# The first modulation split by column halves, and a reordered last head pair in two attention stages

## The reference, cut to what matters

```python
def _modulate(xn, shift, scale):
    return xn * (1.0 + scale) + shift
# first block: x and its context h, both 256 x 1024
ml = (jax.nn.silu(c) @ ada_w[l] + ada_b[l]).reshape(B, N_MOD, 1, D)      # 9 vectors of 1024
x = x + 0.5 * ml[:, 2] * _swiglu(_modulate(_rms(x, ffn1_norm[l]), ml[:, 0], ml[:, 1]), ffn1_w_in[l], ffn1_w_out[l])
...
# second block, twice: attention with 8 heads beside a gated recurrence and merge gates
o_a = nsa_attention(q_a, k_cmp, v_cmp, kv_a[:, :, 2], kv_a[:, :, 3], kv_a[:, :, 4], kv_a[:, :, 5], gates_a, rel_table)
log_a = jax.nn.log_sigmoid((a_lr @ gla_a_w2[l] + gla_a_b[l]).astype(jnp.float32)) / GLA_TAU
o_b = gla_attention(...)
o_b = o_b.reshape(B, S, GLA_HEADS * GLA_DV) * jax.nn.silu(r_b)
gm = jax.nn.sigmoid(g_merge).reshape(B, S, 2, D)
y = gm[:, :, 0] * (o_a @ w_branch_nsa[l]) + gm[:, :, 1] * (o_b @ w_branch_gla[l])
```

## Time and profile before

| what | value |
|---|---|
| median of 3 runs | 2425.76 us (2425.75 to 2430.88) |
| the profiled execution | 2424.43 us |
| its span in the trace | 2422.7 us |
| granted clock, mean | 0.994 |
| PE busy | 2351.5 us, 97% of the span |
| DVE, ACT busy | 1570.5 us (65%), 1162.6 us (48%) |

### The profile page before, as it was taken

The page is one execution under the profiler, slowest core; times in us unless marked ns, Lnnn a source line. Parts: engine busy times, 40 slices in busy tenths (PEclk is TensorE's granted clock), DMA queues, the critical chain, the costliest instruction groups (busy, mean ns, idle before and its releaser), DMA issues.

```text
span 2422.7 us, 33029 instructions
## 1 busy us (share of the span) xinstructions
PE 2351.5 (97%) x13342; PEld 1974.8 (82%) x13342; DVE 1570.5 (65%) x2355; ACT 1162.6 (48%) x1725; POOL 13.0 (1%) x43
## 2 busy tenths in 40 slices
PE   7999999999999999999999998999999999989998
PEld 4887787888888887888888887888888888878887
DVE  4686434656655686667766468676776665766766
ACT  4212323435533345445444478554454446874444
POOL 0000000000000000000000000000000000000000
PEclk9999999999999999999999999999999999999999
DMA  7467322323521224654455643345545555434553
GB/s 301 188 240 267 122 91 103 120 87 124 203 86 57 88 90 164 235 191 174 175 190 191 221 157 140 134 180 191 190 175 191 191 171 217 152 119 164 195 189 137
DMA packets 57920, 399.67 MB, mean 165 GB/s; under 512 B 7789, under 2 KB 8309, under 8 KB 10280
## 3 DMA queue, kind: packets, MB, share of 16 engines
q1 hardware_dynamic: 52704, 383.80, 43.4%
q10 hardware_dynamic: 4272, 10.08, 1.2%
q0 software_dynamic: 800, 3.73, 0.5%
HBM read 396.53 MB, written 2.63 MB: 165 GB/s over the span
## 4 chain that ended last, share of the span: by engine, by line
PE 85%; DVE 6%; ACT 6%; DMA 1%; issue 1%; SPq 0%; DVEq 0%; ACTq 0%
PE pair L506 80%; DMA ring<-in_stream 1%; DVE ring_parts L2294 1%; ACT mix_high L1562 1%; PE pair L901 1%; DVE ring_parts L2284 1%; ACT arena L1912 1%; PE pair L619 1%; PE pair L884 1%; PE pair L1039 1%; ACT ring_high L1549 1%; PE pair L1294 0%; PE pair L848 0%; DVE rows L2411 0%; DVE X L2417 0%
## 5 line engine op out<-in xcount | busy, mean ns | idle before, releaser
L506 PE MATMUL pair<-xT_parts,ring_high 128*128 128x512 f32 x2112 | 747.8, 395 | 4.2 <-DVE ring_parts L2284 1.1
L506 PE MATMUL pair<-xT_parts,ring_parts 128*128 128x256 f32 (+2 forms) x2448 | 694.6, 298 | 7.4 <-DVE ring_parts L2294 4.9
L2284 DVE TENSOR_TENSOR ring_parts<-ring,ring_high 128x2048 fp32r<-128x2048 f32 x194 | 444.1, 2292 | 142.1 <-ACT ring_high L1549 142.0
L506 PEld LDWEIGHTS pair<-xT_parts,ring_parts 128*128 128x128 f32 (+1 forms) x2448 | 461.5, 189 | 51.2 <-issue 12.1
L506 PEld LDWEIGHTS pair<-xT_parts,ring_high 128*128 128x128 f32 x2112 | 384.5, 188 | 81.8 <-DVE ring_parts L2284 2.7
L1549 ACT ACTIVATE ring_high<-ring 128x2048 fp32r<-128x2048 f32 x198 | 377.3, 1909 | 68.2 <-DMA ring<-in_stream 68.2
L2294 DVE TENSOR_TENSOR ring_parts<-ring,mix_high 128x1024 fp32r<-128x1024 f32 x144 | 168.5, 1219 | 77.6 <-ACT mix_high L1562 77.2
L1600 ACT ACTIVATE arena<-pair 128x512 f32<-128x512 f32 x110 | 65.5, 596 | 259.7 <-PE pair L506 259.6
L506 PE MATMUL pair<-ring_parts,xT_parts 128*128 128x512 f32 (+1 forms) x448 | 174.3, 389 | 0.2 <-DVE rows L2524 0.2
L1562 ACT ACTIVATE mix_high<-ring 128x1024 fp32r<-128x1024 f32 x144 | 143.1, 1047 | 61.6 <-DMA ring<-in_stream 57.7
L506 PE MATMUL pair<-ring_parts,g_high 128*128 128x512 f32 x440 | 171.8, 391 | 0.2 <-issue 0.2
(11 more groups left out here) (417 smaller groups left out, 3908.2 us busy)
## 6 DMA issues: line engine op xcount, KB each, us to landing
ring<-in_stream SPq DMA_DIRECT2D x338, 1024.0 KB, 4.8
xn<-in_mods SPq DMA_DIRECT2D x14, 1024.0 KB, 4.9
arena<-in_mods SPq DMA_DIRECT2D x14, 1024.0 KB, 4.9
arena<-in_bT ACTq DMA_DIRECT2D x1, 1536.0 KB, 8.9
bias_scratch<-bias_row POOLq DMA_DIRECT2D x1, 1536.0 KB, 8.3
X<-in_x ACTq DMA_DIRECT2D x1, 1024.0 KB, 11.9
X<-in_ctx ACTq DMA_DIRECT2D x1, 1024.0 KB, 16.4
arena<-in_bT ACTq DMA_DIRECT2D x1, 1024.0 KB, 7.3
```

What stands on the lines that cost most here:

```text
L506: m = pe.matmul(o, l, r, start=start, stop=stop)
L2284: dve.tensor_tensor(out=ring_r[:, slot].rearrange("p a b -> p (a b)"), in0=w, in1=high[:, slot, :], op=ALU.subtract).then_inc(low_ready, 1)
```

## The change

It has two parts that don't touch one another.

**The start.** X and its context are now the first transfers of SP's queue, ahead of the chunks. The first modulation is computed in two column halves, features 0 to 511 and 512 to 1023: four ring chunks hold the first half (two values of k and two of the groups in each), and four chunks of a new tensor, `late`, hold the second, loaded straight into the arena after the ring's fifth chunk. The first two up tiles are repacked so that chunk 0 holds slices 0 to 3 of both and chunk 1 slices 4 to 7 of both. PE runs: three chunks of the first half, slices 0 to 3 of X (`norm_wide`), the fourth chunk, the turn of half 0, slice 4, the first half of up tile 0, the four late chunks, the first half of up tile 1 with the turn of half 1 and the slices 5 to 7 in it, and the second halves of both tiles. ACT and DVE put the second half's work between slices 3 and 4.

**The attention.** In ACT's `beside` the split of a chunk comes after the take and what belongs to it where s is even, where it came before; in odd steps it stays. DVE's `operands` and memset move from step 5 to behind the `maxima` of the last pair.

```diff
@@ SP
+            sp.dma_start(X[:, 0:2, :], t["x"]).then_inc(inputs, 16)
+            sp.dma_start(X[:, 2:4, :], t["ctx"]).then_inc(inputs, 16)
             for j in range(SLOTS):
                 sp.dma_start(ring[:, j], t["stream"][j]).then_inc(loaded[j], 16)
...
+                for j in range(QUAD_LATE) if n == QUAD else ():
+                    sp.dma_start(late_w[j], t["late"][j]).then_inc(late_loaded[j], 16)
@@ PE
             def modulation():
                 pe.wait_ge(consts, FIRST_CONSTS)
                 pe.wait_ge(sc_done, 1)
-                for k in range(KD):
-                    if k == KD - 2:
-                        norm_wide(range(0, 2))
+                for c4 in range(QUAD):
+                    if c4 == QUAD - 1:
+                        norm_wide(range(0, 4))
                     chunk_wait(c.chunk)
-                    quad_part(0, k, ring[:, c.chunk % SLOTS], mod_full if k == KD - 1 else None)
+                    half_part(0, c4, ring[:, c.chunk % SLOTS])
                     owed.append(read[c.chunk % SLOTS])
                     c.chunk += 1
-                quad_turn(0)
+                half_turn(0)
+                norm_wide(range(4, 5))
...
+                def up_first(f, part):
+
+                    low_wait(part)
+                    for k in range(CW * part, CW * part + CW):
...
+                        if (f, k) == (1, 0):
+                            half_turn(1)
+                        if (f, k) == (1, 2):
+                            norm_wide(range(5, 8))
...
+                if nt == 4:
+                    up_first(0, 0)
+                    for j in range(QUAD_LATE):
+                        late_part(j)
+                    up_first(1, 0)
+                    up_first(0, 1)
+                    up_first(1, 1)
@@ ACT
                     for i in range(2):
                         n = 2 * (s % 2) + i
-                        mix_split(l, 16 + 2 * s + i)
+                        if s % 2:
+                            mix_split(l, 16 + 2 * s + i)
                         if s < 2:
                             values(n)
...
                             merge_gate_(n, r2, gm1_sig)
+                        if s % 2 == 0:
+                            mix_split(l, 16 + 2 * s + i)
@@ DVE
+            def second_ready():
+
+                first_half(1)
+                keep_half(1)
+                low(0, 1)
...
-                    elif s == 5:
-                        operands()
-                        step(dve.memset(PlL[:, :, :, :], 0.0))
...
                     for g in range(2):
                         maxima(j, g)
+                    if j == PAIRS - 1:
+                        operands()
+                        step(dve.memset(PlL[:, :, :, :], 0.0))
                     for g in range(2):
                         scale(j, g)
```

More of the change, by code:

```diff
@@ L28 @@
 MOD_STEPS = 18
+QUAD_LATE = 4
 SUMMED_AT = {8: 1, 12: 2, 14: 3, 18: 4}
@@ L291, in build @@
         unit_set = sem("unit_columns_set")
+        late_loaded = mod_loaded + [sem(f"late_modulation_chunk_loaded{i}") for i in range(2)]
         mod_full = sem("modulation_products")
@@ L613, in norm_wide @@
                 for k in slices:
-                    if k == 6 and slices.start:
-                        pe.wait_ge(mod_kept, 1)
+                    if k == 5 and slices.start:
+                        pe.wait_ge(mod_kept, 2)
                     for t_ in range(4):
@@ L703, in up_tile @@
                     steps = [(half, range(KD)) for half in range(2)]
-                    if f == 0 and nt == 4:
-                        steps = [(half, range(k, k + 1)) for k in range(KD) for half in range(2)]
-                    elif f == 0:
+                    if f == 0:
                         steps = [(half, range(k, k + CW)) for k in (0, CW) for half in range(2)]
@@ L1393, in _ @@
             modulation()
-            norm_wide(range(2, 8))
             ffn(4)
@@ L1476, in norm @@
                 for k in range(KD if nt == 4 else 0):
+                    if k == CW and second:
+                        second()
                     c.turned += 1
@@ L2074, in _ @@
             norm(4, "inputs", lambda t_: normA[:, t_ // 2, :], lambda t_: modT[:, 0:8, t_ // 2],
-                 first_modulated)
-            split(0, 1)
+                 first_modulated, second=second_modulated)
             ffn(4)
@@ L2192, in rstds, with norm @@
                     yield t_
-            def norm(nt, ahead=None):
+            def norm(nt, ahead=None, second=None):
                 for t_ in rstds(nt):
@@ L2207, in norm @@
                         high_, whole, low_ = xT_r[:, ks, at - S:at - S + P], xT[:, ks, at:at + P], xT_r[:, ks, at:at + P]
+                    if q == CW and second:
+                        second()
                     dve.wait_ge(x_whole, c.turned + q + 1)
@@ L3200, in add_ffn @@
             order += [(down, FT // 2 - 2), (down, FT // 2 - 1)]
+        if nt == 4:
+            first = np.stack([u.reshape(P, 2, 2 * N) for u in up[0:2]], 2)
+            up[0:2] = [first[:, part].reshape(P, CW, N) for part in range(2)]
         for of, i in order:
@@ L3205 @@
            .transpose(0, 2, 1, 3) for mods in MODS]
-    tiles.extend(ada[0].reshape(-1, P, N))
+    first = np.stack([ada[0][:, h::2] for h in range(2)]).reshape(2, QUAD_LATE, CW, P, N)
+    tiles.extend(first[0].reshape(-1, P, N))
     mods = np.concatenate([a.reshape(-1, CW, P, N) for a in ada[1:]]).transpose(0, 2, 1, 3)
@@ L3209 @@
               .reshape(4, N) for ms in MODS]
+    none = np.zeros((2, N), np.float32)
+    halves_of = [np.concatenate([biases[0][h::2], none]) for h in range(2)]
+    biases = [halves_of[0], biases[1], biases[2], halves_of[1], biases[4], biases[3]]
     pick = np.zeros((P, 2, P), np.float32)
@@ L3268 @@
         "mods": mods,
+        "late": first[1].transpose(0, 2, 1, 3),
         "pick": pick,
```

108 lines of the change are left out of this document (76 added, 32 removed).

## The result

The changed kernel takes 2433.99 us (median of 8 runs, 2432.45 to 2439.56) where the kernel before takes 2426.71 on the same chip: 1.0027 of it, 95% interval 1.0017 to 1.0036, so 4 to 9 us slower. The profiled run has 2433.12 us, the one of before 2424.43. A second set of runs gave 1.0036 (1.0024 to 1.0048). The forecast was 2435.7 with a range of 2428 to 2441. Its difference, 9.9 us, lies a little above the 4 to 9 us of this set and within the 6 to 12 us of the second.

What follows compares the result with a forecast made beforehand. PE, holding 85% of the chain of work, was taken to bound the kernel. Start 3.5 us plus attention 6.4 made 9.9; on 2424.43 that gives 2434.3, and 1.33 for the runs' median makes 2435.7, range 2428 to 2441.

Steps and rivals of the forecast that it cites:

- X earlier: Start: context lands near 8 us, ACT's first square comes at 15.1, the last diagonal at 22.15 instead of 25.74.
- The clock in the slices: Start, PE's slices of X: 13 instructions at 0.47 us, 6.1 us; first half complete at 29.2 instead of 33.65.
- one of my signs of being wrong: Start: the prediction is wrong if PE's records show the clock otherwise than at 27.74 us; no size given.
- The gap ahead of the first up tile: Start: same steps from complete first half to first up product, 7.2 us; first up tile at 36.4, 4.45 earlier.
- the fall of the clock in it: Rival, start: PE's clock falls while idle some 4.3 us before the first up product; 2.8 us more, 2438.5; chance 0.16.
- the sum of the start: Start: the third up tile begins at 66.4 us, 3.5 later than 62.8; bounds +0.5 to +4.6.
- What PE does extra: Start, between the half tiles: late products 4.1 us, second turn 1.06, slices 5 to 7 2.8; together 8.0.
- ACT's order: Attention, steps 2 and 4: splits queue behind the sigmoid; `values` of pair 1 2.0 us later, pair 2 5.5, `output` 4.0.
- DVE's order: Attention, last pair: 6.12 us wait returns as waits for scales and bank; this edit alone gains 0.7 us a layer.
- The sum for a layer: Attention: side pair 7 begins 3.2 us later in each layer, 6.4 in all; bounds of the total 5 to 8.
- Rival 3: Attention: delayed splits stay within DVE's slack, the 6.1 us wait goes; up to 6.1 gained a layer, 2417 us; chance 0.09.

Runs made afterwards that it cites:

- the second profile: The changed kernel run once more, unchanged: its profile spans 2437.0 us, where its first spans 2431.4.
- the start alone: The changed kernel with both edits of the attention undone: ratio 1.0007 to the kernel before (0.9997 to 1.0017).
- the second profile of before: The kernel before run once more, unchanged: ratio 1.0001.
- X first and nothing else: The kernel before with X's two transfers issued first on SP's queue: first up product at 40.97 us instead of 40.85; no total time given.
- the kernel with the split ahead of the sigmoid: The kernel before with both attention edits, but even steps' split between take and sigmoid: attentions 95.40 and 95.39 us, against 95.10 to 95.70 before.
- ACT's order alone: The kernel before with only ACT's edit, in even steps the split behind take and sigmoid: ratio 1.0030.
- DVE's order alone: The kernel before with only operands and memset moved behind the maxima of the last pair: ratio 1.0001.

## Why the prediction was right, step by step

**X earlier.** Right: the last diagonal lies at 21.7 to 22.0 (22.15 forecast), and ACT's first square at 14.9.

**The clock in the slices.** Wrong by 1.75 us: I priced 13 instructions at 0.47, all at the low level. They took 4.44 us, 0.34 each, since the clock rose on the way, and the first half was complete at 27.45, not 29.2. That the records show the clock otherwise than at 27.74 was one of my signs of being wrong. How much otherwise changes with the execution: the same 13 instructions took 5.29 us in the second profile and 5.71 in the start alone. Reading the level from durations where the granted clock says 1.00 was right: the second profile of before shows the same slow chunks, 1.94 us each, at 0.50 from 20 to 28 us.

**The gap ahead of the first up tile.** 7.03 us against 7.2, right: DVE's steps fill it, as in the first profile of before. In that one they ended together with another chain, the landing of the ninth chunk and its split (done at 36.15, the low part begins at 36.26); the second profile of before waits 1.13 us for that split and has a gap of 8.17. But what I gave a chance of 0.16, the fall of the clock in it, is what happened, in both profiles of the changed kernel and, beginning a little ahead of the gap, in that of the start alone. It cost 1.8 us and not 2.8. The Trainium skill (TensorE: Matmul & The Clock Gate, Part 1: The HAM clock gate) says that an idle array goes back to half rate; this trace agrees, 4.09 us of idle and then nine products at 0.43 us. This error and the one before cancel, which is why the sum of the start came out as +2.9 against +3.5. It was partly luck: the second profiles give +4.4 and the start alone +4.9, while the time of the start alone gives +1.7, with nothing at all within its interval.

**What PE does extra.** The late products 3.64 (4.1 forecast), the turn 0.95 (1.06), three slices 2.84 (2.8), together 7.4 against 8.0. PE waits for nothing between the first up product and the slicing that it didn't wait for before. I had the fourth chunk landed before 19 us; with X ahead of it, its products would have begun at 20.99 (X first and nothing else), but they are not needed before 26.4. Right, and the largest term.

**ACT's order.** Right in mechanism and size. `values` of pair 1 lost 2.7 us (2.0 forecast), that of pair 2 6.1 in all (5.5), ACT's `output` is 4.0 us later beyond the start's shift (4.0). The kernel with the split ahead of the sigmoid shows the cause: 5.6 of the 6.1 us go away with it.

**DVE's order.** Right: alone it gains 0.5 to 1.1 a layer (bound 0.7). With ACT's edit the wait of 6.1 us comes back as smaller ones, ahead of the scales (1.52) and the bank (0.90), and side pair 7 begins later as forecast: 86.6 us behind the first `values` in both layers of both profiles, where it was 83.0 to 83.6 before. What the side pair itself then takes depends on the clock, for which the sum had no term.

**The sum for a layer.** 3.0 against 3.2, with 5.0 in the one layer of the second profile where the low clock lasted longer; for the kernel 2.9 + 2 x 3.0 = 8.9 in the profiles, 8.7 by their spans, 7.3 by the medians, against 9.9. Rival 3 (the wait of 6.1 us goes and 12 us are gained) fell at the place named for it: the copies of pair 1 weren't there. But 2.4 to 3.8 us of that wait can be had in each layer, by the order that was changed in the last pair only.

## What to carry to other kernels

When an instruction is moved behind another on an in-order engine, count everything that the other drags along: here the take was 1 us, and the sigmoid behind it 4.6. Change the order only in the step whose wait you have seen: ACT's order alone shortened the last pair by 1.2 to 4.0 us and lost 6.1 in two pairs that had no wait. Work that was hidden in a wait for transfers is plain time once it stands behind the first product, so put it into the idle stretch that the new order opens. Before you move a transfer forward, look which one the first real product waits for, and count the bytes ahead of that one.

## What the runs showed of the hardware that I had not expected

The granted clock falls to half for a few microseconds at five to eight places of every profiled execution behind the start, and not only behind idle time. In the kernel with DVE's order alone it fell during small products (40x40, 64x256 and 40x256), with no idle record before them, and the dense products behind them began at half rate; the kernel before does the same instructions at 477.05 to 481.18 without a fall. The first fence is the former, the second the latter.

```profile
478.42 1.53 PE L506 MATMUL pair<-ident,xn 40*128 40x40 f32 x12
...
481.65 1.91 PE L888 MATMUL pair<-gateB,ident 40*128 40x256 f32 x4
483.49 0.80 PE L506 MATMUL pair<-ring_parts,xT_parts 128*128 128x512 f32 x1
```

```profile
477.05 1.53 PE L506 MATMUL pair<-ident,xn 40*128 40x40 f32 x12
...
480.23 1.02 PE L888 MATMUL pair<-gateB,ident 40*128 40x256 f32 x4
481.18 0.50 PE L506 MATMUL pair<-ring_parts,xT_parts 128*128 128x512 f32 x1
```

Such a fall costs about 1.5 to 3 us: with X first and nothing else, PE is 0.1 us behind the kernel before at the slicing, 3.3 us behind a fall near 480 and 4.8 behind one more near 710. Which places fall changes between executions of one kernel, and spans of the changed kernel differ by 5.6 us, most of it for this. Profiles of two kernels are therefore compared by stretches and not by their spans, with the granted clock of each stretch beside its length.

The other thing is a table load: `sigmoid_rest` spends 2.56 of its 4.6 us on two of them (1.28 each), so a sigmoid by Ln and Exp is a long thing to queue behind.
